# Interleaving the two heads of a pair in a 64-wide attention, on TensorE

## The reference

```python
def global_gqa(q, k, v):
    s = jnp.einsum('bqkgd,bskd->bkgqs', q_blk, k).astype(jnp.float32) * scale
    p = jax.nn.softmax(s, axis=-1).astype(v.dtype)
    return jnp.einsum('bkgqs,bskd->bqkgd', p, v)
# window_gqa_sink: the same, keys within 128 tokens, one sink logit per head in the sum
# mixer_c: the same, keys of a window of rows and 16 columns, a bias per head and offset
```

## Time and profile before

| | |
|---|---|
| three runs | 2623.82, 2616.29, 2624.52 us; median 2623.82 |
| profiled execution | span 2624.0 us from its first to its last instruction; no time of its own is listed beside the span |
| PE, share of the span | 92%, PEld 84% |
| DVE, ACT, POOL | 64%, 40%, 15% |
| attention of layer 0 (heads of 64) | 314.4 to 359.7 us |
| attention of layer 1 (heads of 64) | 1034.0 to 1079.3 us |
| mean granted TensorE clock | 0.951 of full |

### The profile page before, as it was taken

One profiled execution on the slowest core, in us unless ns is written; L12 is line 12 of the kernel. 1 busy time (PEld: TensorE's weight loads), 2 busy tenths in 40 slices (PEclk: granted clock), 3 DMA queues, 4 the chain that ended last, 5 costly groups with the idle time before them and its releaser, 6 DMA issues. The chain is left out here.

```text
span 2624.0 us, 40989 instructions
## 1 busy us (share of the span) xinstructions
PE 2413.6 (92%) x16546; PEld 2212.0 (84%) x16546; DVE 1678.1 (64%) x2403; ACT 1058.3 (40%) x1489; POOL 399.8 (15%) x224
## 2 busy tenths in 40 slices
PE   7998986899999999899997987899999988799997
PEld 7997865799899798688996987797998988797997
DVE  4556765555655635746556889547777788547776
ACT  4334552434333344534344443324444434323433
POOL 0001006100100100101001435320000434420000
PEclk9998997999899999998998989899999989899999
DMA  6554315355455444134552432004554432003553
GB/s 250 188 181 149 141 65 129 115 191 180 156 185 184 160 177 145 65 112 146 192 181 101 172 112 97 1 2 144 189 180 161 176 112 101 13 1 137 178 191 128
DMA packets 52673, 359.81 MB, mean 137 GB/s; under 512 B 6400, under 2 KB 6784, under 8 KB 10944
## 3 DMA queue, kind: packets, MB, share of 16 engines
q1 hardware_dynamic: 46928, 340.81, 36.5%
q0 software_dynamic: 4336, 13.37, 1.8%
q10 hardware_dynamic: 1280, 3.77, 0.4%
HBM read 356.88 MB, written 1.05 MB: 136 GB/s over the span
## 5 line engine op out<-in xcount | busy, mean ns | idle before, releaser
L1409 DVE TENSOR_TENSOR ring_lo<-ring,w_hi 128x1024 fp32r<-128x1024 f32 x600 | 748.1, 1275 | 702.9 <-ACT w_hi L1082 701.7
L1082 ACT ACTIVATE w_hi<-ring 128x1024 fp32r<-128x1024 f32 x648 | 653.9, 1052 | 957.8 <-DMA ring<-weights 788.4
L625 PE MATMUL tile<-xT_hi,w_hi 128*128 128x256 f32 x3136 | 909.0, 290 | 68.8 <-DVE xT_lo L1397 50.3
L625 PE MATMUL tile<-xT_lo,w_hi 128*128 128x256 f32 x3136 | 902.2, 288 | 0.0
L625 PE MATMUL tile<-xT_hi,ring_lo 128*128 128x256 f32 x3136 | 901.8, 288 | 0.0
L625 PEld LDWEIGHTS tile<-xT_hi,w_hi 128*128 128x128 f32 x3136 | 617.0, 197 | 81.6 <-DVE ring_lo L1409 29.4
L625 PEld LDWEIGHTS tile<-xT_lo,w_hi 128*128 128x128 f32 x3136 | 617.5, 197 | 2.1
L625 PEld LDWEIGHTS tile<-xT_hi,ring_lo 128*128 128x128 f32 x3136 | 616.7, 197 | 0.0
L848 PE MATMUL tile<-work 128*128 128x128 f32 (+1 forms) x1600 | 200.8, 290 | 43.6 <-DVE work L1822 40.6
L848 PEld LDWEIGHTS tile<-work 128*128 128x128 f32 x1600 | 195.1, 204 | 51.4 <-DVE work L1822 46.0
L2117 POOL TENSOR_TENSOR x<-work 128x1024 f32<-128x1024 f32 x16 | 47.5, 2988 | 1225.3 <-DVE work L1500 1225.3
(11 more groups left out here) (240 smaller groups left out, 2913.5 us busy)
## 6 DMA issues: line engine op xcount, KB each, us to landing
ring<-weights SPq DMA_DIRECT2D x324, 1024.0 KB, 4.8
work<-ln_g_rows POOLq DMA_DIRECT2D x8, 512.0 KB, 4.2
work<-ln_b_rows POOLq DMA_DIRECT2D x8, 512.0 KB, 4.9
work<-rpb POOLq DMA_DIRECT2D x32, 96.0 KB, 9.3
work<-hmask_in ACTq DMA_DIRECT2D x1, 1408.0 KB, 9.9
x<-x_in SPq DMA_DIRECT2D x1, 1024.0 KB, 7.9
work<-mem_in ACTq DMA_DIRECT2D x1, 1024.0 KB, 7.0
out<-x POOLq DMA_DIRECT2D x1, 1024.0 KB, 4.4
```

Source lines behind the costliest of these rows:

```text
L625: j = mm(ps[:, f * S:(f + 1) * S], w[a][:, k, :], x2[b][:, k, :], start=(k == 0 and i == 0), stop=(k == KT - 1 and i == 2))
L1082: A(high_of(u, h), half_of(ring, u, h), ACT.Copy).then_inc(sems["w_hi"], 1)
L1409: V.tensor_tensor(half_of(ring_lo, u, h), half_of(ring, u, h), high_of(u, h).bitcast(F32), ALU.subtract).then_inc(sems["w_lo"], 1)
```

## The change

The score matmuls of a pair go head 0, head 1, head 0, head 1 (half of the queries by half), and PE waits for the banks of both heads ahead of the first. The value matmuls of a pair go column half 0, 1, 0, 1, and PE waits for the copies of both T tiles ahead of the first. What is computed, the number of instructions on DVE, ACT and POOL and the tile numbers stay. The memory attentions (`per = 1`) keep their order.

```diff
                     if g < groups:
-                        for j in range(per):
-                            e = g * per + j
-                            ps = open_tile(plan.tile[(key, "S", g)] + j)
-                            qs, ks = q_of(e), k_of(e)
-                            for tt in range(TT):
+                        pss = [open_tile(plan.tile[(key, "S", g)] + j) for j in range(per)]
+                        for tt in range(TT):
+                            for j in range(per):
+                                qs, ks = q_of(g * per + j), k_of(g * per + j)
                                 for m in range(len(qs)):
-                                    i = mm(ps[:, tt * S:(tt + 1) * S], qs[m][:, tt * P:(tt + 1) * P],
+                                    i = mm(pss[j][:, tt * S:(tt + 1) * S], qs[m][:, tt * P:(tt + 1) * P],
                                            ks[m], start=(m == 0), stop=(m == len(qs) - 1))
-                            i.then_inc(sems["tile_ready"], 1)
+                                if tt == TT - 1:
+                                    i.then_inc(sems["tile_ready"], 1)
...
                         ps = open_tile(t)
-                        for j in range(2):
+                        for j in range(per):
+                            pe.wait_ge(*taken(plan.tile[(key, "T", g - 3)] + j))
+                        for j, st in [(j, st) for st in range(TT) for j in range(2)] if per == 2 else \
+                                [(j, st) for j in range(2) for st in range(TT)]:
                             e = (g - 3) * per + (j if per == 2 else 0)
-                            pe.wait_ge(*taken(plan.tile[(key, "T", g - 3)] + e % per))
-                            for st in range(TT):
-                                dst = ps[HD * j:HD * (j + 1), 0:S] if per == 2 else ps[:, j * S:(j + 1) * S]
-                                i = mm(dst, v_of(e, j)[:, st, :], probT[:, e % 4, st, :],
-                                       start=(st == 0), stop=(st == TT - 1))
+                            dst = ps[HD * j:HD * (j + 1), 0:S] if per == 2 else ps[:, j * S:(j + 1) * S]
+                            i = mm(dst, v_of(e, j)[:, st, :], probT[:, e % 4, st, :],
+                                   start=(st == 0), stop=(st == TT - 1))
```

## The result

| | before | changed |
|---|---|---|
| median of ten runs | 2624.23 us (2616.29 to 2630.15) | 2634.43 us (2631.01 to 2638.45) |
| span of the profiled execution | 2624.0 us | 2636.7 us |
| attention of layer 0, first score to first projection matmul | 314.48 to 361.29, 46.8 us | 314.74 to 365.63, 50.9 us |
| attention of layer 1, the same | 1034.04 to 1080.86, 46.8 us | 1041.29 to 1096.12, 54.8 us |
| all the rest of the span | 2530.4 us | 2531.0 us |

The ratio to before is 1.004, 95% interval 1.0027 to 1.0053: 10.2 us slower by the medians, where 9 were forecast. The profiled execution of the changed kernel is the slowest of its ten (2638.45 us), so the two profiles lie 12.7 us apart, 2.5 more than the medians.

A forecast was written before the change was run, and what follows sets the result against it. No engine is full: a chain from engine to engine bounds each round, in layer 1 DVE's gapless 4.74 us. Waits of 5.5 (layer 1) and 3.6 (layer 0) sum to +9.1 us on 2624.0, giving 2633 us, range 2625 to 2642.

The forecast's parts named there:

- Nothing to gain from the order: Score and value pairs on PE: the two heads already overlap in listed order, so alternating them changes 0.
- The wait of head 0, layer 1: Layer 1 attention: head 0 now starts when head 1 can; +1.1 us in group 4, +1.48 each in groups 5 to 7.
- the +0.8 that I had priced: Score pair at the lower TensorE clock: 1.96 us against 1.17 for pair and reaction, +0.8 us.
- The wait of head 0, layer 0: Layer 0 attention: the same wait costs +0.2 us in group 3, +1.8 in group 5, +1.6 in group 7.
- Group 6: both heads started together, nothing to lose, 0: Layer 0, group 6: both heads started together at 341.66 in the old profile, so the wait costs 0.
- The value wait: Value matmuls: head 0 also waits for the copy of T1, copied one round earlier; 0, 1 us at most per layer.
- What follows: After the attentions: nothing catches up, so all of the loss passes on to the span.
- The clock: 0: TensorE clock in both attentions: low stretches as likely to move as to multiply; 0, bounds -1.5 and +3.2 us.
- the fourth rival: The clock falls: with more idle time, layer 1 goes to the lower level; +12.3 us, 2636 us, chance 0.15.
- the second rival: Absorbed: slack in some counted rounds or a better clock leaves about half, 2629 us; chance 0.28.
- the fifth: Nothing: the two waits end together in practice and no pass moves; 2624 us, chance 0.06.
- The third rival: Faster: alternating gives each score and value pair about 0.8 us; -16 us, 2608 us, chance 0.06.

The follow-up runs named there:

- the forced 2.21 us: Kernel of before, but PE starts the value matmuls of head 1 only when those of head 0 have ended: 2628.59 us, ratio 1.0005.
- the clock held up: The change plus two 128x512 matmuls into an unread accumulator bank at the end of each step in the two attentions: 2632.13 us, ratio 1.0025.

## Why the prediction was right, and where it was off

**Nothing to gain from the order.** Right, and shown three ways: by the unchanged 1.13 and 1.08 us, by waiting together in the old order (1.14 us), and by the forced 2.21 us. The rule that I cited from the Trainium skill (TensorE: Matmul & The Clock Gate, Part 3) would have the column halves and the heads in listed order one behind the other; these runs contradict it for fp32 matmuls of this shape, with 8 passes in 1.09 us in listed order against 2.21 us when they are one behind the other.

**The wait of head 0, layer 1: +5.5.** Right in mechanism and in size; what came on top was the clock. The round was forecast at 6.22 us and is 6.28. By group, the forecast was +1.1, +1.48, +1.48 and +1.48; the rows give +1.15 (6.28 less 5.13), +2.47 (7.58 less 5.11), +1.55 and +1.53, in sum 6.7. The odd one is the round that ends with a score pair at the lower clock, 2.08 us in place of 1.13, so that DVE stopped for 2.39 us and not for 1.45. Without these 0.94 us the four rounds give 5.8. A further 1.3 us came behind the last scores, where the clock fell once more (transposes of 1.91 us at 1087.49). The low pair is the +0.8 that I had priced and set to 0. All in all this attention grew by 8.0 us in the profiles (46.8 to 54.8). The forecast had named about 51 us in place of 45, counted to the end of the value products; so counted it is 53.4 (1041.29 to 1094.73).

**The wait of head 0, layer 0: +3.6.** The total of this profile, +4.1, is near, but in part by luck. By group the profiles give +1.0, -0.9, +2.8, -0.3 and +1.5 us for groups 3 to 7, where +0.2, nothing (group 4 is not in the count), +1.8, 0 and +1.6 were forecast. Group 5 took 1.0 more than forecast with its score pair at the lower clock (2.04 us at 336.59). I took group 6 for free because its heads started together in the one execution that I had; that round lasted 8.15 us there, most of it at the lower clock, and what it lost to the clock it could not lose again to the wait. At the upper clock the heads are apart in group 6 as well (value part alone): the three rounds to groups 5, 6 and 7 last 5.02, 5.47 and 5.40 us there and 6.92 each with the change and the clock held up, +4.9 in sum, where 3.4 was forecast. These are two profiles of kernels that differ in more than the wait. The step that was mis-sized is "Group 6: both heads started together, nothing to lose, 0".

**The value wait: 0.** Right, 0.9996 (0.9981 to 1.0011). **What follows: all of it passes on.** Right, the span outside the attentions is 2530.4 and 2531.0 us.

**The clock: 0.** Too low. The lower level lasted 17.1 in place of 6.8 us in layer 1 and 23.9 in place of 20.5 in layer 0. One pair of profiles proves little here, but the others fall in line: over both attentions the lower level lasted 41.0, 37.6 and 37.6 us in the three kernels with the merged wait in the old banks and without added matmuls (the change, score part alone, waiting together), and 27.3, 17.1 and 17.0 us in three without it (before, value part alone, column halves kept apart). This is the fourth rival in part: it happened on top of the forecast, for 17.1 of the 54.8 us of layer 1. Its size in the medians stays open, since the change with the clock held up differs from the score part alone by 2.1 us only, less than the intervals hold apart.

**The sum.** 9.1 forecast, 10.2 measured by the medians, 12.1 in the two attentions by the profiles, 8.1 and 9.2 by the medians of the two experiments with the same wait. The interval of the ratio, 7.1 to 13.9 us, rules out the second rival's 5 and the fifth's 0; it holds the forecast's 9.1 and the fourth rival's 12.3 alike, and only the rows tell these apart: rounds of 6.28 us with a stop of 1.45 us at the upper clock. The third rival fell with the result, and with the unchanged lengths of the pairs in every run. (The prediction's highest time, 2624 + 13.3 + 4, is 2641 and not 2642.)

## What to carry to other kernels

Before an order is changed so that work overlaps, compare the time of two in a row with that of one alone in the trace: the hardware may do it already. When waits are merged ahead of a batch, the batch starts with the latest of them; ask which consumer lived on the early half. Where two producers share a ring of buffers, number the buffers by kind, so that an early-released one does not stand behind a late one.

## What the runs showed that was not expected

DVE once stopped for 0.46 us between line 1586 and line 1593 with no other engine named as the cause, at 1057.49 in before and at 1065.96 in the changed kernel, both in group 4. What causes it stays open:

```profile
1065.96 0.69 DVE L1594 TENSOR_REDUCE mx<-work 128x2 f32<-128x512 f32 x1 [0.46 <-DVE work L1587]
```

The same score order took 46.8 us for the attention of layer 0 in one execution (granted clock 0.78, in the profile of before) and 41.2 us in another (clock 1.00, in the value part alone), 5.6 us apart, more than the 4.1 us that the change cost in this attention.

Matmuls listed four passes apart in PE's program run side by side when they use different halves of the array, by rows as well as by columns: 8 passes in 1.14 us (scores) and 1.09 us (values), against 2.21 us for either when the second head came late (scores) or was kept back (values).
